# Latent attention by pairs of heads in a three-mixer network, on one core

## What is computed

```python
c_q, c_kv, k_pe, fq, fk, fv, f_logit = jnp.split(z, ...)        # 384, 256, 32, 512, 512, 512, 8
q = (rms_norm(c_q, g_cq) @ w_uq).reshape(b, l, 8, 96)
kv = (rms_norm(c_kv, g_ckv) @ w_ukv).reshape(b, l, 8, 64 + 64)
k_nope, v_mla = kv[..., :64], kv[..., 64:]
k = jnp.concatenate([k_nope, jnp.broadcast_to(k_pe[:, :, None, :], (b, l, 8, 32))], axis=-1)
q = rope_tail(rms_norm(q, g_q_mla), cos, sin)                    # norm over 96, rotation of the last 32
k = rope_tail(rms_norm(k, g_k_mla), cos, sin)
o_mla = blocked_causal_attention(q, k, v_mla, 96 ** -0.5)        # softmax over the keys up to the query
# forget heads: q, k of 64, the same attention with a sum of log gates added to the scores
# recurrent heads: q_a = l2_norm(q_a) * 128 ** -0.5;  k_a = l2_norm(k_a);  then chunks of 64
```

## Time and profile before

| | |
|---|---|
| median of 3 runs (lowest to highest) | 1845.43 us (1840.47 to 1848.12) |
| the profiled execution, its own time | 1850.25 us |
| its span, first to last instruction | 1848.4 us |
| PE busy | 1768.9 us, 96% |
| DVE, ACT, POOL busy | 884.7, 667.8, 146.4 us |
| chain that ended last, share on PE | 90% (L439, the dense products: 69%) |
| forget heads | 124 to 203 us |
| latent stage, latent heads | 203 to 231, 231 to 406 us |
| differential heads, start of the recurrent heads | 1559, 1657 us |

### The profile page before, as it was taken

The page is one execution under the profiler, slowest core; times in us unless marked ns, Lnnn a source line. Parts: engine busy times, 40 slices in busy tenths (PEclk is TensorE's granted clock), DMA queues, the critical chain, the costliest instruction groups (busy, mean ns, idle before and its releaser), DMA issues.

```text
span 1848.4 us, 26817 instructions
## 1 busy us (share of the span) xinstructions
PE 1768.9 (96%) x11011; PEld 1512.1 (82%) x11011; DVE 884.7 (48%) x1256; ACT 667.8 (36%) x1124; POOL 146.4 (8%) x149
## 2 busy tenths in 40 slices
PE   7999789889999999999999999999999999789998
PEld 7997455569999999999987888888877887567987
DVE  5534244336434343465556434343566368434462
ACT  5423355532413131321133323232335355552222
POOL 1000000004000000050004000000141000003200
PEclk9999898979999999999999999999999999877999
DMA  5220000012222222222222222333355761001001
GB/s 175 92 72 1 1 1 1 17 53 89 92 90 95 90 94 88 93 88 91 92 96 91 92 91 91 94 104 98 104 80 79 85 96 28 1 11 46 1 24 69
DMA packets 127515, 129.19 MB, mean 70 GB/s; under 512 B 7091, under 2 KB 124970, under 8 KB 127422
## 3 DMA queue, kind: packets, MB, share of 16 engines
q1 hardware_dynamic: 127228, 127.82, 25.0%
q10 hardware_dynamic: 194, 0.06, 0.0%
HBM read 125.78 MB, written 2.10 MB: 69 GB/s over the span
## 4 chain that ended last, share of the span: by engine, by line
PE 90%; ACT 4%; DVE 4%; issue 1%; SPq 1%; DMA 0%; ACTq 0%; DVEq 0%
PE ps L439 69%; PE ps L1178 2%; PE ps L997 1%; PE ps L781 1%; PE ps L2108 1%; PE ps L1859 1%; PE ps L2118 1%; PE ps L1184 1%; PE ps L2115 1%; PE ps L892 1%; PE ps L1136 1%; PE ps L779 1%; PE ps L2135 0%; PE ps L2143 0%; PE ps L1829 0%
## 5 line engine op out<-in xcount | busy, mean ns | idle before, releaser
L412 ACT ACTIVATE w_hi<-raw 128x1024 fp32r<-128x1024 f32 (+1 forms) x227 | 239.4, 1055 | 824.9 <-PE ps L439 817.6
L439 PE MATMUL ps<-x_hi,w_hi 128*128 128x258 f32 (+4 forms) x1640 | 450.7, 327 | 3.6 <-DVE x_lo L459 2.7
L439 PE MATMUL ps<-x_lo,w_hi 128*128 128x258 f32 (+4 forms) x1640 | 444.4, 323 | 0.0
L439 PE MATMUL ps<-x_hi,w_lo 128*128 128x258 f32 (+4 forms) x1640 | 443.4, 323 | 0.0
L420 DVE TENSOR_TENSOR w_lo<-raw,w_hi 128x1024 fp32r<-128x1024 f32 (+1 forms) x227 | 295.0, 1300 | 97.3 <-ACT w_hi L412 97.3
L439 PEld LDWEIGHTS ps<-x_hi,w_hi 128*128 128x128 f32 (+2 forms) x1640 | 273.4, 188 | 34.6 <-issue 3.8
L439 PEld LDWEIGHTS ps<-x_lo,w_hi 128*128 128x128 f32 (+2 forms) x1640 | 272.5, 188 | 28.0 <-issue 2.4
L439 PEld LDWEIGHTS ps<-x_hi,w_lo 128*128 128x128 f32 (+2 forms) x1640 | 272.1, 188 | 25.8
L439 PE MATMUL ps<-a_hi,w_hi 128*128 128x258 f32 (+1 forms) x1024 | 282.1, 327 | 6.3 <-DVE gdn_LB L2307 3.2
L439 PE MATMUL ps<-a_hi,w_lo 128*128 128x258 f32 (+1 forms) x1024 | 281.8, 326 | 0.0
L439 PE MATMUL ps<-a_lo,w_hi 128*128 128x258 f32 (+1 forms) x1024 | 281.6, 326 | 0.0
(11 more groups left out here) (380 smaller groups left out, 1895.9 us busy)
## 6 DMA issues: line engine op xcount, KB each, us to landing
raw<-in_w_mlp_up SPq DMA_DIRECT2D x32, 1024.0 KB, 5.4
raw<-in_w_mlp_down SPq DMA_DIRECT2D x32, 1024.0 KB, 5.2
raw<-in_w_in SPq DMA_DIRECT2D x16, 1024.0 KB, 8.9
...
```

Of the source, the lines that this page charges most:

```text
L412: act.activation(dst, panel_view(p)[:, :, o:o + w], ACT.Copy).then_inc(w_hi_ok, 1)
L439: ins = pe.matmul(pair_of_banks[t % 2][0:m, b, 0:c], w[:, k, :], x[:, k, x0:x0 + c], start=(k == order[0] and n == 0), stop=(k == order[-1 ...
```

## The change

Names are those of the code; lines of the new code are written as "new L...".

**Latent weights.** `w_ukv` and `w_uq` are loaded in four and six DMAs that pack columns: all heads' key parts (8 x 64), all value parts, all query parts without rotation, all rotated query parts (8 x 32). They are split into high and low parts during forget pairs 1 and 2 (`mla_weights_act`, `mla_weights_dve`); the rotated query weights are written twice side by side, so that each head's 32 rows appear twice.

**Latents.** Squares and their sums ("lat" steps), Ln, Exp, scaling and splits are moved out of the latent stage into forget pairs 0 to 3.

**Projections.** Twelve steps of 128 rows take the place of sixteen of 96 or 64: "pq" 0 to 3 (queries, two heads a step), "pr" 0 to 3 (rotated parts, two heads doubled), "pk" 0 to 3 (keys), each of three fp32r products per piece of the latent. The common key part is rotated once ("kr"), the queries' by pairs ("rot").

**One inverse root.** The squares of all heads are summed by products with 8-column tables into rows of one tile ("sum" 0 to 7 for the queries, 8 to 12 for the keys; new L1152). One Ln and Exp of 8 rows serves all queries, one all keys; the result is split, and a product with a 0/1 table spreads it over a pair's rows ("bq", "bk").

**Scores and values.** The latent heads then run as pairs 4 to 7 of the forget heads' functions: s, sm, nt, u, pm, pv. Their first scores have five terms where the forget heads have four, the turned ones six where they have four. Probabilities are no longer transposed or divided. The whole `Phase` code is gone.

**Second block.** In `dif_ring` the two "ln" steps of a pair stand further apart; squares are taken one pair ahead, keys before queries, and the scale has two separate tiles. The gate rows are transposed inside the last pair. `gdn_pe` begins before the last output is done: keys are transposed first, then the last "ot", then values; ACT scales all keys, makes the last split, then scales the values.

**Small loads.** Gain vectors of the latent heads are loaded in several copies; three tables are added on SP's queue, two unused ones are dropped.

On PE at the end of the forget values, before and after. The names: `prob`, `v_one` are probabilities and values, `tmp` the squares of the latents, `lat_hi`, `lat_lo`, `uq_hi`, `uq_lo` the splits, `mla_sq` the squares of the heads.

The core of the diff:

```diff
-                  ("g_cq", 3), ("g_ckv", 2), ("gdn_norm_w_2", 1), ("subln_w_2", 1), ("g_q_mla", 1), ("g_k_mla", 1),
+                  ("g_cq", 3), ("g_ckv", 2), ("gdn_norm_w_2", 1), ("subln_w_2", 1), ("g_q_mla:nope", 1), ("g_q_mla:rope", 1), ("g_k_mla", 1), ("g_k_mla:nope", 1),
...
+        body = [("u", c, 0), ("s", c + 1, 3), ("u", c, 1), ("lat", c - 1), ("s", c + 1, 2), ("u", c, 2), ("s", c + 1, 1), ("u", c, 3),
+                ("s", c + 1, 0), ("sm", c + 1), ("pm", c), ("nt", c + 1), ("pv", c)]
+        out += [x for x in body if x[1] < (2 if x[0] == "lat" else 4)]
+    out += [("pq", 0), ("pq", 1), ("sum", 0), ("pq", 2), ("sum", 1), ("pq", 3), ("sum", 2), ("pr", 0), ("sum", 3), ("pr", 1), ("sum", 4), ("rot", 0),
+            ("pr", 2), ("sum", 5), ("rot", 1), ("pr", 3), ("sum", 6), ("rot", 2), ("pk", 0), ("sum", 7), ("rot", 3), ("pk", 1),
+            ("sum", 8), ("pk", 2), ("sum", 9), ("pk", 3), ("sum", 10), ("kr", 0), ("kr", 1), ("sum", 11), ("sum", 12), ("bq", 4), ("v", 0),
+            ("bk", 4), ("v", 1), ("v", 2), ("bq", 5), ("s", 4, 3), ("s", 4, 2), ("bk", 5), ("s", 4, 1), ("s", 4, 0), ("sm", 4), ("nt", 4)]
+    for c in range(4, 8):
+        body = [("u", c, 0), ("s", c + 1, 3), ("u", c, 1), ("bq", c + 2), ("s", c + 1, 2), ("u", c, 2), ("bk", c + 2), ("s", c + 1, 1), ("u", c, 3),
+                ("s", c + 1, 0), ("sm", c + 1), ("pm", c), ("nt", c + 1), ("pv", c)]
+        out += [x for x in body if x[1] < 8]
...
+    out = [("nt", 0), ("s", 1, 3), ("s", 1, 2), ("u", 0, 0), ("ln", 0), ("s", 1, 1), ("u", 0, 1), ("s", 1, 0), ("u", 0, 2), ("ln", 1), ("u", 0, 3),
+           ("pv", 0, 0), ("nt", 1), ("pv", 0, 1)]
     for c in range(1, 4):
-        body = [("u", c, 0), ("s", c + 1, 3), ("u", c, 1), ("ln", 2 * c), ("s", c + 1, 2), ("u", c, 2), ("ln", 2 * c + 1), ("s", c + 1, 1),
-                ("u", c, 3), ("ot", c - 1), ("s", c + 1, 0), ("pv", c, 0), ("nt", c + 1), ("pv", c, 1)]
-        out += [x for x in body if x[1] < 4 or x[0] == "ln"]
-    return out + [("rows", 0), ("ot", 3)]
+        body = [("u", c, 0), ("s", c + 1, 3), ("ln", 2 * c), ("u", c, 1), ("s", c + 1, 2), ("u", c, 2), ("ln", 2 * c + 1), ("s", c + 1, 1),
+                ("u", c, 3), ("rows", 2 * c), ("ot", c - 1), ("s", c + 1, 0), ("pv", c, 0), ("nt", c + 1), ("pv", c, 1)]
+        out += [x for x in body if x[1] < 4 or x[0] == "ln" or x == ("rows", 6)]
+    return [x for x in out if x[0] != "rows" or x[1] == 6] + [("ot", 3)]
...
+        def rope_parts(c, x, q0, nq, k0, nk):
+            r, i = fox_rows(x), c - 4
+            return ((rq_hi[i][r, q0:q0 + nq], rk_one[i][r, k0:k0 + nk]), (rq_lo[i][r, q0:q0 + nq], rk_two[i][r, k0:k0 + nk]))
...
+            last = 3 if c < 4 else 5
...
+                    if n < 3:
+                        q, k = ((qh, kh), (qh, kl), (ql, kh))[n]
+                    elif n == last:
+                        q, k = shift_rows[fox_rows(x), q0:q0 + nq], f_rows[fox_rows(x), k0:k0 + nk]
+                    else:
+                        q, k = rope_parts(c, x, q0, nq, k0, nk)[n - 3]
...
+            for c in range(8):
+                if c == 4:
+                    out_hi(3)
+                    mla_prep_act(act)
                 probs(c, 0)
-                if c:
+                if c not in (0, 4):
                     out_hi(c - 1)
-                for j in range(1, 4):
-                    probs(c, j)
+                if c == 0:
+                    latent_squares_act(act, 0)
+                probs(c, 1)
+                if c == 0:
+                    latent_squares_act(act, 1)
+                if c == 1:
+                    latent_scale_act(act, 0)
+                    mla_weights_act(act, 0)
+                if c == 2:
+                    latent_scale_act(act, 1)
+                    mla_weights_act(act, 1)
+                if c == 3:
+                    latent_hi_act(act)
+                probs(c, 2)
+                if c in (4, 5):
+                    mla_q_hi(act, c - 2)
+                probs(c, 3)
+                if c in (4, 5):
+                    mla_k_hi(act, c - 2)
...
+        def mla_project(pe, slot, w, k0):
+            for k, (hi, lo) in enumerate(w):
+                for n, (a, b) in enumerate(((hi, lat_hi[k0 + k]), (hi, lat_lo[:, k0 + k, :]), (lo, lat_hi[k0 + k]))):
+                    for bank, wd, x0 in halves(LEN):
+                        ins = pe.matmul(slot[:, bank, 0:wd], a, b[:, x0:x0 + wd], start=(k == 0 and n == 0), stop=(k == len(w) - 1 and n == 2))
+            return ins
...
+        def mla_sums(pe, n):
+            bank = pair_of_banks[3]
+            if n == 0:
+                pe.wait_ge(fx["o_done"], 4)
+                pe.wait_ge(s_tab1, 48)
+            if n == 8:
+                pe.wait_ge(mq["ln"], 1)
+            if n < 12:
+                pe.wait_ge(mq["squares"], n + 1)
+                table = sum_table[:, PROJ[n][1] + (4 if PROJ[n][0] == "pr" else 0), :]
+                x = m_sq[n % 2][:, :]
+            else:
+                table, x = tab["ones"][96:P, 0:8], rn_f[96:P, :]
+            for b, wd, x0 in halves(LEN):
+                ins = pe.matmul(bank[0:8, b, 0:wd], table, x[:, x0:x0 + wd], start=(n in (0, 8)), stop=(n in (7, 12)))
+            ins.then_inc(mq["sums"], 1)
...
+        def mla_prep_dve(dve):
+            def raw_saved(kind, c):
+                fox_full(dve, kind, c)
+                row = c + (4 if kind == "pk" else 0)
+                dve.tensor_copy(like(z[:, row, :], LEN), in_psum(fox_bank(kind, c), LEN)).then_inc(mq["raw"], 1)
+            for c in range(4):
+                raw_saved("pq", c)
+            for c in range(4):
+                if c == 3:
+                    raw_saved("pk", 0)
+                mla_rope_dve(dve, c)
+            raw_saved("pk", 1)
+            mla_inverse_lo(dve, 0)
+            raw_saved("pk", 2)
+            raw_saved("pk", 3)
+            mla_key_rope_dve(dve)
+            dve.wait_ge(mq["roped"], 5)
+            mla_q_normed(dve, 0)
+            mla_inverse_lo(dve, 1)
+            mla_q_lo(dve, 0)
+            mla_k_normed(dve, 0)
+            mla_q_normed(dve, 1)
+            mla_k_lo(dve, 0)
+            dve.wait_ge(mq["cleared"], 2)
...
+            l2_square(0)
+            l2_square(1)
             for c in range(4):
                 probs(c, 0)
+                l2_inverse(2 * c)
                 if c:
                     one(c - 1)
-                l2_square(2 * c)
                 probs(c, 1)
-                l2_square(2 * c + 1)
                 if c:
                     unit(c - 1)
                 else:
                     rows_act(act, 0)
                 probs(c, 2)
-                l2_inverse(2 * c)
+                l2_inverse(2 * c + 1)
+                probs(c, 3)
                 if c:
-                    l2_inverse(2 * c + 1)
-                    probs(c, 3)
                     hi(c - 1)
-                else:
-                    probs(c, 3)
-                    l2_inverse(2 * c + 1)
+                if c < 3:
+                    l2_square(2 * c + 2)
+                    l2_square(2 * c + 3)
                 if c == 1:
                     rows_act(act, 2)
             one(3)
             unit(3)
-            hi(3)
+        def dif_last_act(act):
+            dz.wait(act, "o_gated", 4)
+            act.activation(a_hi[:, 7, 0:SEQ], d_out[:, :], ACT.Copy).then_inc(dz.s["out_hi"], 1)
...
-            dz.wait(pe, "l2_normed", 8)
+            dz.wait(pe, "l2_normed", 4)
+            dz.wait(pe, "exp", 16)
             for h in range(GH):
                 for j in range(4):
                     ins = pe.transpose(pblk(A_bank(h), j), qk_a(4 + h)[:, j * P:(j + 1) * P], tab["ident"][:, :])
                 ins.then_inc(gd.s["turned"], 1)
+            dif_step_pe(pe, ("ot", 3))
+            dz.wait(pe, "o_two", 4)
+            for h in (0, 2, 3, 1):
+                if h == 1:
+                    dz.wait(pe, "o_gated", 4)
                 for j in range(4):
                     ins = pe.transpose(pblk(B_bank(h), j), va[:, h, j * P:(j + 1) * P], tab["ident"][:, :])
-                ins.then_inc(gd.s["turned"], 1)
+                ins.then_inc(gd.s["turned_v"], 1)
+            dz.wait(pe, "l2_normed", 8)
             pe.wait_ge(s_tab3, 16 * 7)
             for h in range(GH):
-                gd.wait(pe, "scaled", 2 * h + 1)
+                gd.wait(pe, "scaled", h + 1)
...
+            src = W["w_ukv"][0].rearrange("(k q) (h x) -> q k h x", q=P, x=P)
+            for k in range(2):
+                for x in range(2):
+                    dst = ukv[:, k, 512 * x:512 * x + 512].rearrange("q (h x) -> q h x", x=64)
+                    sp.dma_start(dst, src[:, k, :, 64 * x:64 * x + 64]).then_inc(w_landed[pan % 2], 16)
             sp.wait_ge(w_lo_ok, panels[pan]["first"])
-            sp.dma_start(uq, W["w_uq"][0].rearrange("(k q) n -> q k n", q=P)).then_inc(w_landed[(pan + 1) % 2], 16)
-            mla.wait(sp, "raw", 8)
-            mla.wait(sp, "raw_k", 8)
```

(7 more changed lines are left out.)

827 lines of the change are left out of this document (377 added, 450 removed).

## The result

| | before | after |
|---|---|---|
| median of the runs (lowest to highest) | 1844.97 us (1840.47 to 1848.12) | 1818.38 us (1815.71 to 1820.16) |
| the profiled execution, its span | 1850.25, 1848.4 us | 1817.29, 1815.5 us |

The ratio is 0.9849 (95% interval 0.983 to 0.9868): 26.6 us faster, where 58 were forecast. The time lies above the stated range of 1760 to 1812 us.

The account below looks back on a forecast made before the run. TensorE, busy for 96% of the span, was taken as the bound. Gains of 41.4 us (latent stage) and 18 (second layer), less 0.8 at the start, made 58.6 us: 1787 us against the median, range 1760 to 1812 us.

Parts of the forecast that it names:

- term B: Second layer, differential heads and join to the recurrent heads: 18 us gained, from 8 to 26.
- Join: From the last differential values to the end of the key products: 35.1 us before, 9 us gained.
- rival (5): Second layer: moved sums wait in other places and nothing is gained there, 1805 us; chance 0.07.
- Term A: Latent stage, end of forget values to output projection: 161.5 us against 202.9, 41.4 us gained, from 20 to 59.
- A1: Latent work put into the forget heads: 11.8 us added, 4.8 if PE's run-ahead covers the blocks.
- A2: Preparation, end of forget values to pair 4's first u step: 70.7 us of work, waits and lower clock.
- A3: The four latent pairs: 72 us, including 2.5 us of waits and 2 us of clock.
- A4: Tail, PE's wait ahead of the output projection: 7.0 us, against 3.13 before.
- Start: Kernel start: three more small loads on SP's queue delay the first weight split, 0.8 us lost.
- (1): Rival, latent preparation: ACT and DVE set the pace as projections wait for copies and squares, 1807 us; chance 0.20.
- (3): Rival, latent weights: the loads in short pieces land late, 1792 us; chance 0.05.
- (4): Rival, latent preparation and pairs: handovers put PE on 1.2 GHz; at mean clock 0.6, 1872 us; chance 0.03.

Follow-up runs that it names:

- e3_sums_only: Changed kernel with the new order of square sums kept, but gate rows after the last value products and the old join: 1803.26 us (0.9768 of before).
- e10_x2_early: Changed kernel with gate rows after the last values, new join kept, DVE scaling keys first and between the last output's steps: 1802.24 us (0.9774 of before).
- e5_chains_short: Changed kernel with three first-block handovers shortened: latent splits later, first query copies and squares earlier, first key pair normalized earlier: 1802.37 us (0.9757 of before).

## Why the forecast was wrong

**The step that failed is term B, the second layer.** It was forecast as 9 us in the differential heads and 9 in the join.

- *Differential heads.* "These 13.1 us go" was right: no sum waits any more. In pairs 0 to 2 it brought 4.7 us. Of the 9.3 us of waits for sums there 3.20 stayed in pair 0 as a wait of the value products for exponentials (3.4 forecast), and 1.9 us more than before came in smaller waits, for exponentials, maxima and an inverse root; the clock gave back 0.5. In pair 3 the wait for the last inverse root was forecast as 3.8 us and measured 3.14. What I left out is the transposes that I moved there: I took their 4.5 us off the join and added them nowhere. Behind the wait they cost 7.0 us, and the value products behind them 6.7 instead of 5.1 (in `e3_sums_only`, without the rows and behind the same wait, 6.9). The pair became 5.8 us longer: 24.6 against 18.8.
- *Join.* I wrote that PE would be through the key products "at about +24 to +26" and "still waits twice there at the lower clock". It did wait twice, 3.88 and 1.31 us. The price was the failure: the sum has at most 2 us for it, as it takes a gain of 9 out of "9 to 11". The 16 us of decay products behind the second wait ran at half clock to their end, and cost 7.5 us more than in `e3_sums_only`. Result 35.1 us, not 26. (The "33 us" that I gave for this stretch before is a slip; its own numbers give 35.1.) Without the waits the count was good: in `e10_x2_early`, which has the new join with the gate rows in it, the key products end 26.7 us after the values.
- Even without these two faults the term was too large. In `e10_x2_early` the second block is 11.7 us shorter than before: 8.5 in the join, where 9 were forecast, and 4.4 in the differential heads, where 9 were, with 1.2 lost behind the key products.
- The term was said to lie between 8 and 26 us. No rival had it below zero; rival (5) stopped at nothing gained.

**Term A was right in its mechanism and short by 5 us.** A1: the sums took 4.99 us (4.8 forecast) and the added waits are some 7.6 us (7.0: my 2.8 in pair 1 measured 2.06, and in pair 3, where I had 2.8 more than before, it was 5.65 against 1.43); the lower clock behind them, 4 us, wasn't in the sum. A2: waits 11.3 us (12.8), of which the first sum's is 4.28 (4.5) and pair 4's 4.10 (5.1); but 64.0 us of work and clock against 57.9. In `e5_chains_short`, with 3.9 us of waits and a clock of 0.99, the same work took 59.5 us. So the lower clock cost 4.5 us, where I had 2.5, and PE's work, which I had counted as 55.4 us, was 4.1 us short. A3: 67.5 us instead of 72; the 2.5 us of waits and 2 of clock that I had added did not come, as DVE kept pace: the pairs stand 20.0, 18.3 and 17.2 us apart. A4: 7.06 (7.0). Start: 2.1 us here; over this kernel and the eleven others with the new first block the mean is 1.0 (0.8 forecast).

**The cut weights were hidden**, as taken. They landed long before ACT's first split of them, which follows its own exponential without a gap (the issues: size, us to landing; then ACT):

```profile
ukv<-in_w_ukv SPq DMA_DIRECT2D x4, 256.0 KB, 4.4
uq<-in_w_uq SPq DMA_DIRECT2D x3, 256.0 KB, 3.8
```

```profile
167.94 0.65 ACT L1033 ACTIVATE mla_sq<-mla_sq 128x528 f32<-128x528 f32 x1
168.50 1.47 ACT L1058 ACTIVATE uq_hi<-uq 128x1536 fp32r<-128x1536 f32 x1
```

256 KB in short pieces took 3.8 to 4.4 us, 1152 KB in long ones 5.4: per byte three to four times as long. With the rule of the Trainium skill, "DMA: Bandwidth & Descriptors", section Specifications, on transfers under 512 bytes, the trace agrees in direction at most: the loads differ in size too (64 KB took 1.9 us), and no run changes the pieces alone. The time was not touched, since the last issue was at 133 us and the first use at 168.5.

**The rivals.** (1), paces of ACT and DVE, did not come: the projections follow one another without a wait. (3), late weights, did not come either; its 5 us stand on no row, the rows gave 3. (4), the clock, was the right mechanism at the wrong place. I looked for it in the 128 us of the preparation and the pairs, where the mean came out at 0.90 (I had called under 0.85 a refutation), and asked only from which point it would turn the whole into a loss. My argument against it, that "the dense stretches run at 0.98 with waits of this size", was a misreading: the forget heads before had waits of 0.18 to 1.25 us, and behind the longest the value products took 7.21 us. The clock should have been priced wait by wait. The signs: forget heads 16.6 us longer (8 to 14 said), first sum's wait 4.28 (4 to 6), output projection at 371.5 us (364), key products' end 33.8 us earlier (59). None of the three things that I had named as showing me wrong came (preparation 75.3 us, pairs at most 20.0 apart, clock 0.90): all three look at the first block, and the forecast failed in the second.
